# Expert weights in nine slots instead of six, TensorE's pair loop in rounds of three pairs, and a reordered entry and end of the expert stages

## The reference

```
for l in (0, 1):
    x = x + hybrid_mixer(rmsnorm(x))                  # mix0, mix1
    h = rmsnorm(x)                                    # moe0, moe1
    grp     = argmax(h @ w_rg + b_rg)                 # 4 groups of 8 experts
    experts = top 2 of (h @ w_re + b_re) in that group, gates = p_grp * softmax(top 2)
    x = x + sum over the 2 of gate * (silu(h @ w_gate[e]) * (h @ w_up[e])) @ w_down[e]
x = rmsnorm(x)                                        # final
```

## Time and profile before

| what | value |
|---|---|
| median of 3 runs | 2272.11 us (2271.2 to 2273.15) |
| the profiled execution | 2272.86 us, span 2271.0 us |
| granted TensorE clock, mean | 0.971 |
| TensorE matmuls busy | 2110.4 us (93% of the span) |
| VectorE, ScalarE busy | 769.3 us (34%), 628.4 us (28%) |
| moved by DMA | 598.92 MB, mean 264 GB/s |
| chain that ended last | TensorE 65%, DMA 28%, of it `w_expert_up` 27% |

### The profile page before, as it was taken

How to read it: one execution, slowest core, us unless ns; L and a number is a source line. 1 busy time by engine, 2 the same in 40 slices (tenths; PEclk the granted TensorE clock), 3 DMA queues, 4 the chain that set the end, 5 groups by cost and what they waited for, 6 DMA issues and landing times.

```text
span 2271.0 us, 28397 instructions
## 1 busy us (share of the span) xinstructions
PE 2110.4 (93%) x11978; PEld 1432.7 (63%) x11978; DVE 769.3 (34%) x1125; ACT 628.4 (28%) x902; POOL 35.7 (2%) x53
## 2 busy tenths in 40 slices
PE   6989899999979899999999799989999999999998
PEld 4744444444447444444444699879989995666997
DVE  1431111111124311110111555465566552375555
ACT  2311111111123111111111433343343342364333
POOL 5000000000000000000000000000000000000000
PEclk9989999999989899999999899999999999999999
DMA  9429999999963299999999763546355534504530
GB/s 271 173 88 420 422 422 423 423 421 421 413 233 112 74 412 423 423 423 422 422 422 416 279 223 101 186 167 222 104 220 186 185 129 162 216 7 149 187 116 32
DMA packets 142459, 598.92 MB, mean 264 GB/s; under 512 B 6913, under 2 KB 22337, under 8 KB 126002
## 3 DMA queue, kind: packets, MB, share of 16 engines
q1 hardware_dynamic: 139730, 592.01, 66.7%
q0 software_dynamic: 2656, 5.86, 1.1%
HBM read 596.80 MB, written 1.05 MB: 263 GB/s over the span
## 4 chain that ended last, share of the span: by engine, by line
PE 65%; DMA 28%; DVE 4%; issue 1%; ACT 1%; SPq 0%; DVEq 0%; ACTq 0%
DMA ring<-in_w_expert_up 27%; PE PS L987 20%; PE PS L863 12%; PE PS L1001 10%; PE PS L723 4%; PE PS L1074 3%; PE PS L774 3%; PE PS L974 2%; PE PS L713 2%; PE PS L874 1%; PE PS L1227 1%; PE PS L852 1%; DMA ring<-in_w_in 1%; DVE x L1701 1%; PE PS L697 1%
## 5 line engine op out<-in xcount | busy, mean ns | idle before, releaser
L863 PE MATMUL PS<-ring,xs 128*64 128x512 f32 x2048 | 462.6, 605 | 59.2 <-DMA ring<-in_w_expert_up 57.3
L863 PEld LDWEIGHTS PS<-ring,xs 128*64 128x64 f32 x2048 | 159.5, 139 | 355.9 <-issue 352.9
L1255 ACT ACTIVATE split<-ring 128x2048 fp32r<-128x2048 f32 x132 | 253.1, 1920 | 424.6 <-PE PS L987 268.0
L1725 DVE TENSOR_TENSOR split<-ring,split 128x2048 fp32r<-128x2048 f32 x132 | 302.4, 2293 | 176.9 <-ACT split L1255 171.8
L987 PE MATMUL PS<-hT_high,split 128*128 128x256 f32 x2560 | 329.1, 281 | 0.0
L987 PEld LDWEIGHTS PS<-hT_high,split 128*128 128x128 f32 x2560 | 316.5, 189 | 2.8
L1001 PE MATMUL PS<-split,ffn_hid 128*128 128x512 f32 x1056 | 246.9, 390 | 0.0
L874 PE MATMUL PS<-ring,work 128*64 128x512 f32 x1024 | 226.8, 595 | 0.0
L1001 PEld LDWEIGHTS PS<-split,ffn_hid 128*128 128x128 f32 x1056 | 195.5, 188 | 39.0
L987 PE MATMUL PS<-hT_low,split 128*128 128x256 f32 x1280 | 178.3, 282 | 0.0
L987 PEld LDWEIGHTS PS<-hT_low,split 128*128 128x128 f32 x1280 | 163.6, 189 | 0.0
(11 more groups left out here) (284 smaller groups left out, 1628.0 us busy)
## 6 DMA issues: line engine op xcount, KB each, us to landing
ring<-in_w_expert_gate SPq DMA_DIRECT2D x64, 2048.0 KB, 17.4
ring<-in_w_expert_up SPq DMA_DIRECT2D x64, 2048.0 KB, 17.7
ring<-in_w_expert_down SPq DMA_DIRECT2D x64, 2048.0 KB, 14.4
ring<-in_ffn_w_gate SPq DMA_DIRECT2D x20, 2048.0 KB, 7.9
ring<-in_ffn_w_up SPq DMA_DIRECT2D x20, 2048.0 KB, 9.0
ring<-in_ffn_w_down SPq DMA_DIRECT2D x20, 2048.0 KB, 7.8
ring<-in_w_in SPq DMA_DIRECT2D x8, 2048.0 KB, 18.7
ring<-in_nsa_w_in SPq DMA_DIRECT2D x5, 2048.0 KB, 9.2
```

The lines of the kernel that those rows point to most:

```text
L863: last = pe.matmul(PS[e * CAP:(e + 1) * CAP, bank, :], xs[:, k, e * CAP:(e + 1) * CAP], view((r + e) % RING, KT, DE)[:, k, :], start=(k == ...
L1255: return act.activation(o, i, ACT.Copy)
L1725: v.tensor_tensor(at[:, 1], src, at[:, 0], ALU.subtract).then_inc(S.ffn_low, 1)
```

## The change

Nine slots hold expert weights: the six of the ring and three in the first 12288 columns of the work area. The areas that the expert stage itself needs, and the mixer's oT, yg and sqa, move behind them (`EXPERTS_AT`, 12288 in place of 8192). `slot_order` puts the three after the first four ring slots. SyncE fills all nine ahead of the loop; the first of the three waits for `mix_ss`. Then it refills a slot for load i once load i - 9 is used. Six loads make a pair and nine slots a turn, so slots repeat every three pairs: the loops on SyncE (4 rounds of 18 loads) and on TensorE (4 rounds of pairs 2, 3, 4, then the last two passes written out) have three pairs as their body. The expert loads have semaphores of their own.

Inside a pair, `down` signals each of its two column halves, and y_high, y_low and the final combine go by halves. The last pair has no gather. In pair 0 the gate product waits for xs half by half. At the entry each half of x has its own root and is scaled on its own. `keep_clock` puts twelve and four float32r matmuls into bank 0 around the rank products. At the end TensorE loads the flag without a wait for the addition, which is now made for each half of the tokens. VectorE makes the first low half of ffn00 ahead of the addition in moe1 and the second behind the final norm. ScalarE loads the table for the root ahead of the mixers and of the final norm.

```diff
+SLOTS = 9
...
-        EXPERTS_AT = 2 * 2 * HALF
+        EXPERTS_AT = (SLOTS - RING) * 4096
...
+        def slot_of(r, k):
+
+            if r < RING:
+                return ring[:, r, :].rearrange("p (k n) -> p k n", k=k)
+            return work[:, (r - RING) * 4096:(r - RING + 1) * 4096].rearrange("p (k n) -> p k n", k=k)
+
+        def slot_order(first):
+
+            at = [(first + j) % RING for j in range(RING)]
+            return at[0:4] + list(range(RING, SLOTS)) + at[4:6]
...
             def moe_loads(l):
-                for which, e in PAIR:
-                    load(cols(0, 4 if which == "down" else KT, D if which == "down" else DE),
-                         expert_src(l, e, which), pair_used(M, which), 1 - e)
-                per = {M.gate_done: 1, M.up_done: 1, M.down_done: 1}
-                with sp.Fori(1, PAIRS) as p:
-                    w.enter(p, per, first=1)
-                    pair_loads(l, M, 2 * p, True, w)
-                    w.leave(PAIRS - 1)
-                for which, e in PAIR:
-                    free.append((pair_used(M, which), 1 - e, None))
-                n[0] += RING
+                order = slot_order(n[0])
+
+                def fill(i, pair):
+                    which, e = PAIR[i % 6]
+                    r = order[i % SLOTS]
+                    sp.dma_start(slot_of(r, 4 if which == "down" else KT), expert_src(l, 2 * pair + e, which)) \
+                        .then_inc(M.loaded[r], 16)
+
+                def refill(i, pair):
+
+                    which, e = PAIR[(i - SLOTS) % 6]
+                    if e == 0:
+                        sp.wait_ge(pair_used(M, which), w.to(pair_used(M, which), signals(which)))
+                    fill(i, pair)
+
+                if l:
+                    w.past(M.down_done, 2)
+                for i in range(SLOTS):
+                    if order[i] < RING:
+                        s, m, over = free[n[0] - RING]
+                        sp.wait_ge(s, w.to(s, m))
+                        n[0] += 1
+                    elif order[i] == RING:
+                        sp.wait_ge(S.mix_ss, w.to(S.mix_ss))
+                        w.past(S.mix_ss)
+                    fill(i, i // 6)
+                with sp.Fori(0, 4) as q:
+                    w.enter(q, {M.gate_done: 3, M.up_done: 3, M.down_done: 6})
+                    for i in range(SLOTS, 3 * SLOTS):
+                        refill(i, q * 3 + i // 6)
+                    w.leave(4)
+                for i in range(9 * SLOTS, 6 * PAIRS):
+                    refill(i, i // 6)
+                for which, m in (("gate", 1), ("gate", 0), ("up", 1), ("up", 0), ("down", 2), ("down", 0)):
+                    free.append((pair_used(M, which), m, None))
...
+                def wide(bank, slots, halves=False):
+
+                    for r in slots:
+                        pe.wait_ge(s.loaded[r], f.to(s.loaded[r], 16))
                     for k in range(KT):
+                        if halves and k % 4 == 0:
+                            pe.wait_ge(s.x_made, f.to(s.x_made))
                         for e in range(2):
                             last = pe.matmul(PS[e * CAP:(e + 1) * CAP, bank, :], xs[:, k, e * CAP:(e + 1) * CAP],
-                                             view((r + e) % RING, KT, DE)[:, k, :], start=(k == 0), stop=(k == KT - 1))
+                                             slot_of(slots[e], KT)[:, k, :], start=(k == 0), stop=(k == KT - 1))
...
+                def down(slots, last_pair):
+                    for r in slots:
+                        pe.wait_ge(s.loaded[r], f.to(s.loaded[r], 16))
                     for c in range(2):
-                        pe.wait_ge(s.x_made, f.to(s.x_made))
+                        if not last_pair:
+                            pe.wait_ge(s.x_made, f.to(s.x_made))
                         for k in range(4):
                             for e in range(2):
                                 last = pe.matmul(PS[e * CAP:(e + 1) * CAP, 6 + c, :], EB.hT[:, k, e * CAP:(e + 1) * CAP],
-                                                 view((r + e) % RING, 4, D)[:, k, c * 512:(c + 1) * 512],
+                                                 slot_of(slots[e], 4)[:, k, c * 512:(c + 1) * 512],
                                                  start=(k == 0), stop=(k == 3))
-                    last.then_inc(s.down_done, 1)
-
-                def combine(start, tokens=range(TT)):
+                        last.then_inc(s.down_done, 1)
...
-                def one_pair(p):
-
-                    behind = p is None or p > 0
-                    wide(4, (first) % RING).then_inc(s.gate_done, 1)
+                def one_pair(p, last_pair=False):
+
+                    behind = p > 0
+                    slots = where(p)
+                    wide(4, slots[0:2], halves=(p == 0)).then_inc(s.gate_done, 1)
                     if behind:
                         pe.wait_ge(s.marks_made, f.to(s.marks_made))
-                    wide(5, (first + 2) % RING).then_inc(s.up_done, 1)
+                    wide(5, slots[2:4]).then_inc(s.up_done, 1)
                     if behind:
-                        pe.wait_ge(s.y_made, f.to(s.y_made))
+                        pe.wait_ge(s.y_made, f.to(s.y_made, 2))
                         combine(p == 1, (0,))
                     pe.wait_ge(s.h_made, f.to(s.h_made))
                     for k in range(4):
...
                     for t in range(TT):
                         last = pe.transpose(PS[:, 5, t * P:(t + 1) * P], EB.OHg[:, t, :], ident)
                     last.then_inc(s.oh_turned, 1)
-                    pe.wait_ge(s.onehot, f.to(s.onehot))
-                    gather()
+                    if not last_pair:
+                        pe.wait_ge(s.onehot, f.to(s.onehot))
+                        gather()
                     pe.wait_ge(s.hT_made, f.to(s.hT_made))
-                    down((first + 4) % RING)
-
-                first = n[0]
+                    down(slots[4:6], last_pair)
...
                 one_pair(0)
                 one_pair(1)
-                per = {s.onehot: 1, s.x_made: 2, s.marks_made: 1, s.y_made: 1, s.h_made: 1, s.onehot_g: 1, s.hT_made: 1}
-                per.update({s.loaded[r]: 16 for r in range(RING)})
-                with pe.Fori(2, passes) as p:
-                    f.enter(p, per, first=2)
-                    one_pair(None)
-                    f.leave(passes - 2)
+                per = {s.onehot: 3, s.x_made: 6, s.marks_made: 3, s.y_made: 6, s.h_made: 3, s.onehot_g: 3, s.hT_made: 3}
+                for p in range(3):
+                    for r in where(p):
+                        per[s.loaded[r]] = per.get(s.loaded[r], 0) + 16
+                rounds = (passes - 3) // 3
+                with pe.Fori(0, rounds) as i:
+                    f.enter(i, per)
+                    for p in range(2, 5):
+                        one_pair(p)
+                    f.leave(rounds)
+                for p in range(2 + 3 * rounds, passes):
+                    one_pair(p, p == passes - 1)
                 pe.wait_ge(s.marks_made, f.to(s.marks_made))
                 pe.wait_ge(s.y_made, f.to(s.y_made))
-                combine(False).then_inc(s.combined, 1)
+                combine(False, range(TT), (0,))
+                pe.wait_ge(s.y_made, f.to(s.y_made))
+                for t in range(TT):
+                    combine(False, (t,), (1,)).then_inc(s.combined, 1)
+
+            def keep_clock(n_):
+
+                for _ in range(n_):
+                    pe.matmul(PS[:, 0, :].rearrange("p (s k) -> p s k", s=4), ident_r[:, :],
+                              ident_r[:, :].unsqueeze(1).to_broadcast([P, 4, P]), start=True, stop=True)
 
             def moe(l):
                 transpose_x(f"moe{l}", 0)
...
                                          start=(k == 0), stop=(k == KT - 1))
                 last.then_inc(S.routed, 1)
 
+                keep_clock(12)
                 pe.wait_ge(S.marked, w.to(S.marked))
                 pe.matmul(PS[:, 6, 0:NE], upper, EB.mk[:, 0, :], start=True, stop=True)
                 pe.matmul(PS[:, 6, NE:2 * NE], ones, EB.mk[:, 0, :], start=True, stop=False)
...
                 pe.matmul(PS[:, 6, 2 * NE:3 * NE], ones, EB.mk[:, 0, :], start=True, stop=False)
                 pe.matmul(PS[:, 6, 2 * NE:3 * NE], ones, EB.mk[:, 1, :], start=False, stop=True) \
                     .then_inc(S.ranked, 1)
+                keep_clock(4)
...
-                experts(M, w, PAIRS, y_high[l])
-                n[0] += RING * PAIRS
+                order = slot_order(n[0])
+                experts(M, w, PAIRS, y_high[l], lambda p: [order[(6 * p + j) % SLOTS] for j in range(6)])
...
-                pe.wait_ge(S.moe_added, w.to(S.moe_added))
                 most = pe.value_load(flag[0:1, l:l + 1], min_val=0, max_val=SEQ)
...
+                act.wait_ge(S.set_up, 1)
+                table_for_roots()
...
-                    take_x()
+                    if not last_pair:
```

(40 more changed lines are left out.)

70 lines of the change are left out of this document (35 added, 35 removed).

## The result

The changed kernel takes **2218.02 us** (median of 4 runs, 2216.85 to 2221.96), beside 2271.65 for the kernel before in the same session: a ratio of 0.9768, 95% interval [0.9754, 0.9782]. The forecast was 2217. Its profiled execution took 2221.96 with a span of 2220.1, so it is the longest of the four, and the two profiles differ by 50.9 us where the medians differ by 54.1 (2272.11 - 2218.02).

A forecast was written before the change was run, and what follows sets the result against it. The expert pair loop was taken as bound by bytes at 422 GB/s. Savings of 2 x 21.8 + 6.0 + 5.2 = 54.8 us from the 2272.11 us median gave 2217 us, own range 2209 to 2227.

The forecast's parts named there:

- Nine slots: Expert stages: three more loads landed when the stream starts, 87 left instead of 90, saving 14.9 us per stage.
- Last pair without gather: Last expert pair: without the gather, down starts 0.2 us after the last landing, not 3.6, saving 3.4 us per stage.
- Entry: Start of each expert stage: three items bring the first gate product 3.5 us earlier per stage, bounds -0.3 and 4.8.
- (a): Stage entry: scaling the first half of hp ahead of the hT copies brings the logits 1.4 us earlier, bounds 0 and 2.0.
- (b): Stage entry: keep_clock's fillers hold TensorE's clock through idle time, so the gather gets 1.5 us shorter; bounds 2.1, or 0.3 lost.
- (c): Stage entry: the first gate product starts after half of xs, saving 0.65 us.
- Behind moe0: Exit of moe0: flag read straight behind combine and work done in halves start the next transposes 6.0 us earlier.
- Behind moe1: Exit of moe1: ScalarE's earlier high parts and the reordered split subtractions start ffn00's hT_high 5.2 us earlier, bounds 2 and 7.
- At nothing: Table loads at the start of mix0 and mix1 counted as zero gain; removed flag_f copies counted in the tail.
- Rival 1: Pair loop's three taken back-jumps per stage stall TensorE 7.2 us each: 2228 us, or 2242 if leaving pays too; chance 0.08.
- Rival 2: Whole change: only fewer loads and the dropped last gather pay, 36.6 us in all, giving 2235 us; chance 0.15.
- Rival 3: Expert loads: nine in flight, a third into the shared work area, slow the stream to 381 GB/s: 2309 us; chance 0.03.

The follow-up runs named there:

- e1: Changed kernel with six ring slots for the experts instead of nine, everything else kept: 2250.18 us.
- e2: Changed kernel with nine slots, but the first fills of the last three held until the first gate product: 2248.30 us.
- e12: Changed kernel with nine slots, but the first fills of only the last two held until the first gate product: 2238.48 us.
- e7: Changed kernel with the gather kept in the last pair: 2225.77 us.
- e6: Changed kernel with TensorE waiting for the complete x before loading its flag, as before the change: 2227.43 us.
- e10: Changed kernel with TensorE's flag loaded behind pair 0 of the stage, leaving only the jump behind combine: 2219.74 us.
- e4: Changed kernel without the twelve and four filler matmuls: 2221.44 us.
- e5: Changed kernel measured again without an edit, as reference for its group: 2219.3 us.
- e3: Changed kernel with VectorE's old entry order, both hT copies first, then both halves of hp scaled: 2219.54 us.
- e8: Changed kernel with VectorE scaling the first half of hp inside the mixer, between its two last adds, and the second behind the hT copies: 2214.44 us.
- e9: e8 with 24 and 10 filler matmuls in place of 12 and 4: 2215.35 us.
- e11: e8 plus the fillers of e9, the early flag load of e10, and ScalarE making ffn00's second high half behind the final norm, against the changed kernel: 2211.64 us.

## Why the prediction was right, step by step

The time came out 1 us from the forecast, but that closeness is luck: two terms were off in opposite directions. The two entries brought 3.3 us less than the sum has for them (in the mean of many), the exit of moe0 2.5 more.

**Nine slots, 14.9 a stage: right.** From the first `gate` product to D the profiles give 18.5 and 17.7, for 14.9 + 3.4 = 18.3. e1 and e2 give 32.2 and 30.3 for the three loads in two stages, forecast 29.8, and e12 20.5 for two of them, forecast 19.9.

**Last pair without gather, 3.4 a stage: right.** 6.2 for both in the traces of e7, and 0.14 us from landing to `down`.

**Entry, 3.5 a stage: the term that was mis-sized, and in it item (a).** In the profile of the changed kernel it is -1.4 and +0.6, in place of 3.5 each; so D of moe0 was 605.35 and not 600.3, and this is the largest part of what the profile lacks against the sum. The kernels whose entry has the changed kernel's code (the two measurements of it, e1, e2, e6, e7, e10 and e12) show 16 entries from 20.2 to 25.6 us, in the mean 22.5, against 24.15 and 24.44 in the one profile of before: 1.8 us a stage.

These 16 can be cut by item, counted from the end of the last addition to x. The gather starts 16.5 us behind it in the mean (14.9 to 17.4), before 16.2: (a), forecast at 1.4, brought -0.2. The gather takes 4.5 in the mean (3.81 in ten entries, 5.2 to 6.7 in six), before 5.7 and 6.0: (b), forecast at 1.5, brought 1.3. The `gate` product follows the gather at once, before 0.7 behind it: (c), forecast at 0.65, brought 0.8. So (a) is the step that failed. It counted VectorE's steps and took the router's products at the speed that they had. With the scaling in front of the hT copies these products run as 8 and 24 with a wait of 0.67 us between. In 14 of the 18 entries with this order (the two of e4 with them) the 24 took 4.6 to 5.3 us, at a granted clock down to 0.50; in the other four they took 2.9 to 3.0, as in e5:

```profile
138.77 2.87 PE L994 MATMUL PS<-wr,hT 128*128 128x36 f32 x24 [0.67 <-DVE hT L1756]
...
150.71 3.81 PE L892 MATMUL PS<-work,hp 128*128 128x128 f32 x32 [1.55 <-DVE work L1965]
```

There the gather starts 14.9 behind x, 1.3 less than before, so (a) is there, and the entries are 20.23 us, where the steps gave 24.15 - 3.5 = 20.65. In the kernels with all 32 products in one group (before, e3, e8, e9, e11) they took 3.73 in nine entries of ten, and 5.58 in the first of e3. So the low clock goes with the new order, though not with it alone; what brings it down is not shown.

Item (b) came near its size, but its reason doesn't hold: it took the gather at a low clock for a result of the idle time ahead of it alone. The rows show the clock down before that, under the router's products and the fillers themselves. Without fillers (e4) the gather takes 5.8 and 6.7 us, but with the same twelve and four it takes 5.0 to 6.5 in all four entries of e3 and e8, so they don't hold the clock by themselves. By their times, e3 for (a) and e4 for (b) give 1.5 us and 2.1 to 3.4 us for two stages, where 2.8 and 3.0 stood in the sum; neither is told apart from a half or a double of it, and (c) has no experiment. e9 shows the remedy: with no wait of over 0.2 us between the router's products and the gather the clock was 1.00 throughout and all four entries of e9 and e11 took 19.5.

**Behind moe0, 6.0: the order was right, the size was not.** It brought 8.5. TensorE's first transpose came at D + 15.9, for D + 16.7: the step took combine to end at D + 9.5 and 7.2 us from there, and they are D + 9.9 and 6.0 (615.22 to 621.21). The other 1.7 is a second stop among the 16 transposes that the kernel before has behind the twelfth:

```profile
644.81 2.82 PE L697 MATMUL PS<-cst,x 128*128 128x128 f32 x12 [9.61 <-issue]
649.46 0.66 PE L697 MATMUL PS<-cst,x 128*128 128x128 f32 x4 [1.83 <-issue]
```

and the changed kernel hasn't. Nothing in the change removes it on purpose, and I did not see it. e6 shows that the place of the flag is worth 7 to 8 us in all, more than was forecast for it, as it shortens the exit of moe1 too; there it is a part of the next term.

**Behind moe1, 5.2: right**, 4.8 by the profiles. The chain goes as written, over the wait of ScalarE for `ffn_w_up` (landing at 1215.11), the table load, the norm in halves and the last subtraction:

```profile
1215.14 1.91 ACT split L1315
...
1217.07 1.28 ACT L1353
...
1221.78 1.29 DVE x L2369
...
1223.09 2.29 DVE split L1792
1225.38 0.40 DVE hT_high L2128 x2
```

hT_high begins at D + 21.0, forecast D + 20.4, before D + 25.7.

**At nothing:** the changed kernel's profile is shorter by another 1.6 us in mix1 and by 0.8 behind ffn00's start, and no step speaks of them. No experiment was made on them, but the traces show that those in mix1 are no gain of the change: the 24 products of one column near its end and the 16 output products behind them took 3.35 and 9.97 us before, 2.84 and 8.81 after, and the same 16 take 7.1 to 10.2 us in other traces.

**The sum.** Terms of 36.6 + 7.0 + 6.0 + 5.2. By the profiles 36.3 - 0.9 + 8.5 + 4.8 + 2.1 (the rest of the account) = 50.8. With the mean entry in place of that one execution's, 2 x 1.84 = 3.7 for -0.9, it is 55.4, beside the 54.1 of the medians. So the entries alone, 4.5 us above their mean, can account for the 3 us by which the profiled execution is long.

**The waits.** About 10 waits on `up` were forecast and 18 came. The reserve was 16 us, used up at 2.3 a pair; by these two numbers it should have been 7 waits a stage, 14 in all, and not 10. The reserve is 23 us: TensorE alone would reach D at 187.34 + 14 x 27.03 + 13.73 + 2.7 = 582.2, and D is 605.35; and a pair of 27.03 falls behind a stream of 29.8 by 2.8. 23 / 2.8 = 8 pairs before the end TensorE meets the stream, and the trace has 9 waits a stage. What was wrong is the 27.5, with the division, and it costs no time.

**Rival 1, the back-jump stalls: refuted** by the `gate` product at 295.46. By the Trainium skill ("Runtime: NRT & Kernel Launch", Instruction fetch mechanics) a body over two pages of 256 instructions would fetch at each taken branch; 852 instructions of TensorE a round show no such stall, so that the runs speak against it and for the other figure of the same section, room for 2048. **Rival 2, only the bytes: refuted** in its size, since e6 alone shows 7 to 8 us beyond them. **Rival 3, a slower stream: refuted** by the 420 to 424 GB/s with nine loads in flight.

**What stays open.** The second stop of TensorE's transposes, 1.8 us behind the twelfth (before), 4.7 behind the fourth (e7), 2.9 and 2.65 behind the sixth (e9, e11), and none in the other ten traces. It comes at one place in one kernel and at another in the next, though the products are the same, and always as issue and not as a wait for data, behind the jump over the overflow code. That the place of the code in memory decides it is what I take from this; no kernel was run that moves the code and nothing else, so it isn't shown. Open too is why the clock falls in one execution and not in another: the entries of 20.2 us (e5) and 25.6 (the changed kernel's first), the same program, differ by 2.5 in the router's 24 products and 2.9 in the gather, and nsa by 3.3 between traces.

## What to carry to other kernels

In a loop bound by bytes, what can be landed ahead of it is worth its bytes divided by the rate (shown here for two and for three loads a stage, with nine slots and with six): look for room that is idle ahead of the loop. Where an engine takes a data-dependent branch, let it decide as soon as its operand is there and not when the stage is complete, since some 6 us pass between its last product and its next. And a stretch in which TensorE waits in small pieces is an unsteady one: either fill it without a hole or don't count on its clock, and judge an edit of it by several profiles.

## What was not expected of the hardware

- The granted clock fell to 0.50 while TensorE was busy all of the time by the rows, with 24 router products of 36 columns (5.33 us, where e9 took 3.73 for all 32) and with the fillers. Under the router's products it fell in one execution of a kernel but not in another (20.23 us of entry in e5, 25.58 in the changed kernel, the same program).
- A flag load and a jump of TensorE cost 6.0 us from its last product to its next; 0.8 us of it is the load (e10). With a wait for the add ahead of it, 7.45 us (e6) from there.
- Stops of 1.8 to 4.7 us come and go in the stage behind an edited one, at a place among equal instructions that differs from kernel to kernel; in e9 this ate the 2.3 us by which its last `down` came earlier than e8's.
